# Another placement of a group's token rows in the partitions, and the last expert's products issued in the common order

## The reference

```
g_p, g_idx = top_k(softmax(xt @ wg + bg), 1)              # one group of 8
e_val, e_loc = top_k(e_logits[that group], 2)             # two of its 8 experts
y = sum of weight * ((silu(x @ w_gate[e]) * (x @ w_up[e])) @ w_down[e])
out = rms_norm(x + y)
```

## Time and profile before

| | |
|---|---|
| time, median of 3 (lowest to highest) | 1959.36 us (1957.67 to 1960.65) |
| time of the profiled execution | 1959.72 us |
| its span | 1957.9 us |
| mean granted clock of PE | 0.992 of full speed |
| busy share of the span: PE, weight load, DVE, ACT, POOL | 96%, 69%, 36%, 30%, 13% |
| moved by DMA | 505.92 MB |

### The profile page before, as it was taken

The page is one execution under the profiler, slowest core; times in us unless marked ns, Lnnn a source line. Parts: engine busy times, 40 slices in busy tenths (PEclk is TensorE's granted clock), DMA queues, the critical chain, the costliest instruction groups (busy, mean ns, idle before and its releaser), DMA issues.

```text
span 1957.9 us, 28614 instructions
## 1 busy us (share of the span) xinstructions
PE 1871.3 (96%) x11946; PEld 1354.0 (69%) x11946; DVE 706.1 (36%) x1768; ACT 585.2 (30%) x1212; POOL 245.4 (13%) x208
## 2 busy tenths in 40 slices
PE   6999999999999999999999999989989899899996
PEld 5887777777777767788986666556566566655653
DVE  5331223333766668701142232313223123231322
ACT  5323333333544544322312232313113132131312
POOL 2433343333000000144100000000000000000000
PEclk9999999999999999999999999999999999999999
DMA  9554233233322331155589999999999999999994
GB/s 279 138 147 115 70 81 86 65 81 82 62 58 44 74 127 48 44 172 184 213 353 413 427 426 427 428 427 427 426 428 426 427 424 428 425 418 428 420 423 163
DMA packets 177394, 505.92 MB, mean 258 GB/s; under 512 B 52835, under 2 KB 136163, under 8 KB 151147
## 3 DMA queue, kind: packets, MB, share of 16 engines
q1 hardware_dynamic: 174954, 495.63, 66.2%
q0 software_dynamic: 2304, 8.39, 1.1%
HBM read 495.85 MB, written 16.53 MB: 262 GB/s over the span
## 4 chain that ended last, share of the span: by engine, by line
PE 79%; DMA 18%; ACT 1%; DVE 1%; issue 0%; SPq 0%; POOL 0%; POOLq 0%; ACTq 0%; DVEq 0%
PE banks L944 25%; PE banks L1352 12%; DMA at_region<-in_w_up 9%; PE banks L1101 9%; DMA x_region<-in_w_up 8%; PE banks L1377 7%; PE banks L1274 6%; PE banks L1353 3%; PE banks L1081 3%; PE banks L1053 2%; PE banks L1031 2%; PE banks L1323 2%; PE banks L993 1%; PE banks L1192 1%; PE banks L1038 1%; PE banks L1362 1%
## 5 line engine op out<-in xcount | busy, mean ns | idle before, releaser
L944 PE MATMUL banks<-ht_rounded,ring_rounded 128*128 128x512 f32 x1056 | 359.3, 394 | 0.7 <-ACT at_region L1515 0.7
L944 PEld LDWEIGHTS banks<-ht_rounded,ring_rounded 128*128 128x128 f32 x1056 | 195.1, 188 | 53.4 <-issue 13.8
L1352 PE MATMUL banks<-at_region,ht_region 128*64 128x256 f32 x800 | 180.7, 385 | 14.7 <-DMA at_region<-in_w_up 14.7
L848 POOL TENSOR_TENSOR ring_rounded<-ring_region,at_rounded 128x512 fp32r<-128x512 f32 (+1 forms) x92 | 115.9, 1291 | 511.1 <-ACT at_rounded L1454 511.1
L1353 PE MATMUL banks<-at_region,ht_region 128*64 128x256 f32 x768 | 175.4, 388 | 0.0
L2234 DVE SCALAR_TENSOR_TENSOR at_rounded<-banks,small,ring_rounded 128x512 fp32r<-128x512 f32 x128 | 96.1, 750 | 208.5 <-ACT ring_rounded L1740 207.6
L2227 DVE COPY consts<-banks 128x128 f32<-128x128 f32 x64 | 18.7, 292 | 403.7 <-PE banks L1362 403.7
L1352 PEld LDWEIGHTS banks<-at_region,ht_region 128*64 128x64 f32 x800 | 109.8, 139 | 72.7 <-issue 26.8
L1740 ACT ACTIVATE ring_rounded<-banks,small 128x512 fp32r<-128x512 f32 x128 | 88.0, 687 | 240.1 <-PE banks L1377 240.1
L944 PE MATMUL banks<-ht_rounded,at_rounded 128*128 128x512 f32 x352 | 142.7, 405 | 1.0 <-ACT at_region L1507 0.7
L1730 ACT ACTIVATE ring_region<-banks,consts 64x256 f32<-64x256 f32 x64 | 30.1, 470 | 374.6 <-PE banks L1353 374.4
(11 more groups left out here) (297 smaller groups left out, 3483.6 us busy)
## 6 DMA issues: line engine op xcount, KB each, us to landing
at_region<-in_w_gate SPq DMA_DIRECT2D x24, 2048.0 KB, 29.6
at_region<-in_w_up SPq DMA_DIRECT2D x23, 2048.0 KB, 28.8
at_region<-in_w_down SPq DMA_DIRECT2D x22, 2048.0 KB, 24.2
ring_region<-in_w_in SPq DMA_DIRECT2D x36, 1024.0 KB, 6.0
x_region<-in_w_down SPq DMA_DIRECT2D x17, 2048.0 KB, 26.9
x_region<-in_w_up SPq DMA_DIRECT2D x15, 2048.0 KB, 30.0
x_region<-in_w_gate SPq DMA_DIRECT2D x14, 2048.0 KB, 30.8
ring_region<-in_w_gate SPq DMA_DIRECT2D x9, 2048.0 KB, 34.2
```

The source lines that it names most:

```text
L848: ins = nc.gpsimd.tensor_tensor(w_low[n % RING][:, ks, 0:width], ring[n % RING][:, ks, 0:width], w_high[n % 2][:, ks, 0:width].bitcast(F32 ...
L944: ins = mm(out, w[:, k, 0:width], h[:, k, :], start=k == 0 and i == 0, stop=k == KT - 1 and i == 2)
L1352: mm(place[0:CAP, 0:D_EXPERT], x, gate[j], start=j == 0, stop=j == KT - 1)
```

## The change

Two edits. The first gives `row_iota` and `cap_rows` another order. Partition p now holds rank 2 * (p // 16) + p // 4 % 2 + 16 * (p % 4 + 4 * (p // 8 % 2)); the constants table gets 64 columns more. Ranks 0, 1, 2, 3, ... sit in partitions 0, 4, 16, 20, ...; ranks 16, 17, ... in partitions 1, 5, ...; ranks from 64 on in partitions whose number modulo 16 is 8 or more. The second takes the exception of E63 out of the three `group` functions: `gate_up(E63)` now stands ahead of `finish_expert(E62)`, and ACT and DVE follow. `finish_expert(E63)` keeps its own order, and the waits for `piece_in` stay.

```diff
-C_TOK = C_IOTA + P
+C_RANK = C_IOTA + CAP
+C_TOK = C_RANK + P
...
-    c[:, C_IOTA:C_TOK] = np.arange(P)
+    rank = 2 * (p // 16) + p // 4 % 2 + 16 * (p % 4 + 4 * (p // 8 % 2))
+    c[:, C_IOTA:C_RANK] = np.arange(CAP)
+    c[:, C_RANK:C_TOK] = rank
...
-    c[:, C_ROWS:] = np.where(np.arange(P) < CAP, np.arange(P), -5000.0)
+    c[:, C_ROWS:] = np.where(rank < CAP, rank, -5000.0)
...
-        row_iota = consts[:, C_IOTA:C_IOTA + P]
+        row_iota = consts[:, C_RANK:C_RANK + P]
...
                 for e8 in range(PER):                    # PE
-                    if ends_all(c, g, e8):
-                        finish_expert(c, g, e8 - 1, begins)
-                        gate_up(c, g, e8)
-                        continue
                     gate_up(c, g, e8)
...
                 for e8 in range(PER):                    # ACT
-                    if ends_all(c, g, e8):
-                        take_result(c, g, e8 - 1)
-                        gate(c, g, e8)
-                        continue
                     gate(c, g, e8)
...
                         copy_hidT(*before)               # DVE
-                    if ends_all(c, g, e8):
-                        build_spread(*before)
-                        split_result(*before)
-                        hidden(c, g, e8)
-                        continue
                     hidden(c, g, e8)
```

More of the change, by code:

```diff
@@ L55 @@
 MISC = FOX_HEADS + 3 * NSA_HEADS
+CAP = 64
 C_IDENT = 0
@@ L215 @@
         SPLITS[step, 1].append((ALL_TILES + a, part))
-CAP = 64
 PASSES = T // CAP
```

## The result

The changed kernel takes 1964.97 us in the median of 15 runs (1962.17 to 1965.97); the kernel before, run beside it, takes 1960.2 us (15 runs, 1957.51 to 1961.34). The ratio is 1.0025, 95% interval 1.0019 to 1.0032. The change costs some 4.9 us. The forecast was 1959.4 us and no change that can be told; the time lies above its range of 1948.5 to 1963.5.

What follows compares the result with a forecast made beforehand. DMA, moving some 427 GB/s in the experts' stage, was taken to bound the kernel, with PE nearly as full. 1959.72 - 2.75 (placement) - 0.3 (last scatter) + 2.7 (order) = 1959.4 us; range 1948.5 to 1963.5.

Steps and rivals of the forecast that it cites:

- The step that failed: In the experts' weight loads, only engine 0 was taken to bind, its rows falling from 100 to 91.
- the term: Placement, up to the landing of E62's up: nine fewer rows on engine 0 at 0.306 us each, -2.75 us.
- The rows and the partitions: Gathers and scatters: four neighbouring partitions per engine, 32 to 35 sharing with 0 to 3; up to 64 rows on 8 engines.
- The first rival: Gathers and scatters: rows spread over all 16 engines, fullest 61 instead of 100, -11.9 us; 1949.9 us in all, chance 0.14.
- The order of the last expert: End chain: moving gate_up(E63) ahead exchanges one stall for another, +2.7 us, bounds +0.2 to +4.4.
- the waits at the quarters: In gate_up(E63), PE meets a wait of about 0.7 us at each quarter of the weights, up to four times.
- The end of the chain: After down_product(E62), PE waits for E62's second half to be split, 1.55 us after the product; last down product at 1942.1.
- The last scatter: Final scatter of 19 rows: longest chain falls from 4 rows to 3, -0.3 us (0 to -0.6).
- The second one: Placement brings nothing, fullest engine staying at 100 rows; clock falls in last gate_up, order costs 4.4; 1964.1 us, chance 0.12.

Runs made afterwards that it cites:

- E63: Not a run: the last expert of the kernel, whose gate_up the change moved ahead of finish_expert of the expert before it.
- E62: Not a run: the expert before the last; its first matmul comes 928.67 us after a mark ahead of the experts' stage before, 931.46 in the changed kernel.

## Why the prediction was wrong

**The step that failed** is the sentence "The load of the other engines does not bind, since a load counts as landed when its last engine is done." The second half is right. The first half counted the load of an engine in rows alone, and took the engine with most rows for the last one. The engines carry instruction fetches too, at twice a row's price or more for a byte, and unequally. Before, two lower engines were about equally full: one with 100 rows, and engine 5 with 78 rows and six fetches of 16 KB (33.5 us). The change took 9 rows from the former and gave 11 to the latter, 89 in all, or 36.9 us. In place of -2.75 us the term measured +2.8. The lower bound of the term, nothing (-0), left out a loss altogether, and so the range ended at 1963.5.

**Not the upper half.** The mirrored run suggests that the loss comes from the 82 rows that the change put on the upper engines. It does not, or not first: the fullest upper ones are 12 and 13, with 80 rows and at most six fetches, 24.7 + 9.4 = 34.1 us, less than engine 5. From 1070 us to E62 the kernel before has these fetches (queue, packets, MB, share):

```profile
q8 instruction: 44, 0.72, 0.3%
q14 instruction: 10, 0.08, 0.0%
```

44 packets at 1.56 us are 69 us, or 8.6 on each of eight engines. In the kernel before a step with one packet of queue 8 (1547.55 to 1562.23) is 14.68 us: that packet was on an engine with time to spare, hidden. The mirrored kernel has the same in some steps and 16.23 in another.

**A rule that this case limits.** The Trainium skill, page "Runtime: NRT & Kernel Launch", section "Instruction fetch mechanics", says that an engine fetches its instructions in blocks of 16 KiB over a DMA queue of its own, and that crossing a block is "mostly hidden". The packets of queue 8 are of 16 KB here (97 packets, 1.59 MB), those of queue 14 of 8 KB. For the fetching engine "mostly hidden" may hold; no run here tells. For the DMA engine that carries the block it does not: 28 packets of 8 KB cost 11.4 and 12.0 us where that engine was among the fullest, and nothing where it was not.

**The rows and the partitions.** This part was right: blocks of four partitions, the ninth with the first, two halves (the last scatter had nine packets an engine, eight engines empty). The first rival, that the rows really spread over 16 engines, was wrong for this formula. Its price was wrong too: true spreading brings 7.2 us, not 11.9, at E62, and 1952.2 us rather than 1947.2 (1949.9 of the rival less the 2.7 of the order).

**The order of the last expert.** This term was right in place and size: +2.78 (29.51 against 26.73) for +2.7, and 29.45 in the run of the order alone. Of its parts, the waits at the quarters were 0.27 and 0.55, two instead of four of 0.7. E62's `gate_up` began at the lower clock (granted 0.50 of full speed from 1916.46 to 1918.00 us, after PE's wait of 2.60; its first matmul 0.66 us instead of 0.40) and took 8.5 us, from 1916.46 to 1924.97, instead of 7.1. So `gate_up(E63)` began later, and the quarters had come nearer. The end of the chain is as forecast: a wait of 0.83 for DVE's split after `down_product(E62)` and 0.38 for the last copy. In the sum it doesn't matter whether PE waits for the quarters or comes too late for them.

**The last scatter.** Forecast -0.3; from its issue to its landing it took 3.2 us instead of 4.6. The direction was right and the size too small: a chain of four rows and their end packets became one of three, and eight engines instead of five took them. With 1.0 us of a later mark, which differs from run to run (983.8 to 985.7 in all kernels), it about cancels out.

**The rivals.** The second one, *the change costs time*, gave 1964.1 us at a chance of 0.12; the time was 1964.97. Its place was half right: it said that other sharing would leave the placement without gain, and it took the drop of the clock in the last waits for the rest. In truth the sharing was as assumed, the placement did harm, and the clock cost nothing in the sum. The number was met by another mechanism. What speaks against the choice of 0.70 for the forecast is in the prediction itself: excesses of 9.35, 5.44 and 3.57 us were explained with 9.8, 4.9 and 3.67 by rows on engine 0, and that fit was taken for proof that rows are all that engines differ in. It could speak only for one of the fullest engines, and that fit was in part luck, since engine 5 was as full with 22 rows less.

**What stays open.** Which instructions queue 8 fetches, and why its packets go to these eight engines. Whether the second lower engine is 6 or 7. Why the packet behind a fetch takes longer. No run took the rows off engines 5, 6 and 7; that this would bring more than the even order is not shown.

## What to carry to other kernels

Where all loads are striped over 16 DMA engines and the stage is bound by them, the last engine sets the pace, and what sets the last engine is its whole load: rows, and also instruction fetches, which the queue table shows at 0.3% of the span and which look like nothing. A fit of the excess on the fullest engine says nothing of the others; before rows are moved, mirror the placement once and see whether the time stays (here it did not, by 6.2 us), and string the packets of the trace together to see what each engine carries.

Spread indirect rows over all 16 engines: here the even order gives 0.996 of the time (0.9947 to 0.9974), the best of the kernels run, with the last expert's order left as it was. Long runs of instructions on an engine that seems idle are not free in such a stage.

## What the runs showed of the hardware

- A fetch packet of 8 KB costs its DMA engine 0.66 us (0.31 itself, 0.35 more for the packet behind it) and one of 16 KB 1.56 us (1.07 and 0.49), where a row of 8 KB takes 0.31. Steps of 15.34 and 16.22 us instead of 14.69 agree.
- The packets of queue 8 go round eight of the 16 DMA engines, 9 to 13, one of 14 and 15, 5, and one of 6 and 7: five or six on each of eight strings in 830 us, none on the rest.
- 28 packets that were added to POOL's instructions all went to one DMA engine of partitions 0 to 63: 12.0 us in plain order, 11.4 with even rows, nothing beyond the noise (-1.0) with that half of the engines lightly loaded.
- So DMA engines are not equally free: the same rows mirrored from partitions 0 to 63 to partitions 64 to 127 made the last load 6.2 us later in 930.
